# A second output bank, sums by slot, and seven block products for the values of an attention layer

## What is computed

```python
ada = jax.nn.silu(c) @ w_ada[i] + b_ada[i]
sh_m, sc_m, gt_m, sh_f, sc_f, gt_f = [a[:, None, :] for a in jnp.split(ada, 6, axis=-1)]
h = rms_norm(x, g_pre_mix[i]) * (1 + sc_m) + sh_m
y = token_mixer(h, ...)          # proj = h @ w_in; attention || gla; concatenated @ w_out
x = x + gt_m * rms_norm(y, g_post_mix[i])
h = rms_norm(x, g_pre_ffn[i]) * (1 + sc_f) + sh_f
y = hier_moe(h, ...)             # top-1 group, top-2 experts of 32
x = x + gt_f * rms_norm(y, g_post_ffn[i])
```

## Time and profile before

| | us |
|---|---|
| three runs | 1489.6, 1491.54, 1492.07; median 1491.54 |
| the profiled execution, time | 1491.1 |
| its span in the profile | 1489.3 |
| granted TensorE clock, mean | 0.932 |
| busy, of the span | PE 83%, DVE 50%, PEld 37%, ACT 14%, POOL 4% |
| chain that ended last | DMA 38%, PE 34%, SP's queue 17%, DVE 7%, ACT 2% |

### The profile page before, as it was taken

The page is one execution under the profiler, slowest core; times in us unless marked ns, Lnnn a source line. Parts: engine busy times, 40 slices in busy tenths (PEclk is TensorE's granted clock), DMA queues, the critical chain, the costliest instruction groups (busy, mean ns, idle before and its releaser), DMA issues.

```text
span 1489.3 us, 18989 instructions
## 1 busy us (share of the span) xinstructions
PE 1236.6 (83%) x7341; PEld 548.7 (37%) x7342; DVE 748.9 (50%) x1082; ACT 211.6 (14%) x491; POOL 52.5 (4%) x68
## 2 busy tenths in 40 slices
PE   4799999899999999876777677767767779999967
PEld 4687644654444453321222122222222223333322
DVE  5876257678674866443234223422432335555525
ACT  3011121222201041100000000000000001111103
POOL 0000300000110020000000000000000000000010
PEclk9899999999999999989899889988898899999989
DMA  9999979888899789999999999999999999999996
GB/s 354 392 383 385 353 296 379 312 334 302 322 408 386 275 329 392 426 424 428 425 425 427 427 428 424 426 427 427 423 428 426 427 423 428 427 425 426 428 427 269
DMA packets 102004, 583.51 MB, mean 392 GB/s; under 512 B 6656, under 2 KB 31536, under 8 KB 58192
## 3 DMA queue, kind: packets, MB, share of 16 engines
q1 hardware_dynamic: 98752, 572.81, 94.6%
q10 hardware_dynamic: 1664, 6.46, 1.1%
q0 software_dynamic: 1552, 3.75, 0.9%
HBM read 579.30 MB, written 3.69 MB: 391 GB/s over the span
## 4 chain that ended last, share of the span: by engine, by line
DMA 38%; PE 34%; SPq 17%; DVE 7%; ACT 2%; issue 1%; POOL 0%; ACTq 0%; DVEq 0%
DMA stream<-in_w 32%; PE ps L701 8%; SPq L544 6%; PE ps L913 5%; DMA stream<-in_w_ada 5%; SPq L563 4%; PE ps L786 4%; PE ps L967 4%; SPq L538 3%; PE ps L632 3%; SPq L479 2%; PE ps L698 1%; PE ps L874 1%; PE ps L819 1%; DVE wk L1053 1%
## 5 line engine op out<-in xcount | busy, mean ns | idle before, releaser
L913 PE MATMUL ps<-stream,wk 128*32 128x512 f32 x2304 | 323.5, 690 | 132.8 <-DMA stream<-in_w 131.9
L1365 DVE TENSOR_TENSOR acc<-ps,acc 128x2048 f32<-128x2048 f32 x37 | 84.8, 2292 | 430.7 <-PE ps L874 430.7
L913 PEld LDWEIGHTS ps<-stream,wk 128*32 128x32 f32 x2304 | 71.2, 118 | 372.3 <-issue 296.8
L967 PE MATMUL ps<-stream,cst 128*32 128x512 f32 x1152 | 152.1, 656 | 61.9 <-DMA stream<-in_w 61.8
L701 PE MATMUL ps<-stream 128*128 128x512 f32 x448 | 196.6, 594 | 0.3 <-PE ps L632 0.3
L632 PE MATMUL ps<-stream 128*128 128x256 f32 x512 | 120.7, 401 | 1.8 <-ACT stream L1510 1.8
L701 PEld LDWEIGHTS ps<-stream 128*128 128x128 f32 x448 | 83.6, 190 | 99.3 <-issue 99.2
L632 PEld LDWEIGHTS ps<-stream 128*128 128x128 f32 x512 | 102.9, 202 | 17.4 <-issue 1.9
L920 PEld LDWEIGHTS ps<-cst,wk 128*128 128x128 f32 x576 | 70.4, 193 | 62.8 <-issue 62.8
L1053 DVE SCALAR_TENSOR_TENSOR wk<-stream,cc,wk 128x768 f32<-128x768 f32 (+1 forms) x90 | 83.6, 929 | 11.4 <-DMA stream<-in_w_ada 8.8
L874 PE MATMUL ps<-wk,cst 32*128 32x512 f32 x592 | 87.9, 664 | 0.8 <-ACT wk L1681 0.8
(11 more groups left out here) (270 smaller groups left out, 986.5 us busy)
## 6 DMA issues: line engine op xcount, KB each, us to landing
stream<-in_w SPq DMA_DIRECT2D x190, 2048.0 KB, 40.9
stream<-in_w_ada SPq DMA_DIRECT2D x64, 1024.0 KB, 7.0
stream<-in_w_in SPq DMA_DIRECT2D x8, 4096.0 KB, 16.7
stream<-in_w_ada SPq DMA_DIRECT2D x64, 384.0 KB, 10.0
stream<-in_w_out SPq DMA_DIRECT2D x4, 4096.0 KB, 16.3
stream<-in_w_ada SPq DMA_DIRECT2D x16, 512.0 KB, 10.1
stream<-in_w_in SPq DMA_DIRECT2D x4, 2048.0 KB, 13.2
stream<-in_w_in SPq DMA_DIRECT2D x2, 3072.0 KB, 16.2
```

What stands on the lines that cost most here:

```text
L913: last = nc.tensor.matmul(bank(1 + m)[32 * g:32 * g + 32, :], xe[:, k + g, :], w13[m][:, k + g, :], start=(k == 0), stop=(k == KD - 4))
L967: last = nc.tensor.matmul(bank(2)[32 * g:32 * g + 32, :], hid[:, k, :], w2v[:, k, 512 * g:512 * g + 512], start=(k == 0), stop=(k == 3))
L1365: V.tensor_tensor(y4, ps[:, b0:b0 + 4, :], y4, ALU.add).then_inc(ysum_sb, 1)
```

## The change

- **Block products.** `BLOCK_UNITS = [4, 5]`: for each of the two value units the 256 by 2048 by 512 product is made of seven products of 128 by 1024 by 256 (8 matmuls of 256 columns each) in place of eight. TensorE makes two in three of the unit's slots and one in the fourth. VectorE forms four sums of h once (128 by 1024 each), and for each unit four sums of weight blocks (128 by 2048) in place, in the unit's slab, and eight sums of output blocks (128 by 256). ACT copies two of the products.
- **Second output bank.** `o_bank`: the outputs of `att` go to bank 4 and bank 6 in turn, four each, so the wait for `o_sb` before a new group is one group later. `mod_bank` is rearranged to make room.
- **Sums by slot.** `ADA_IN` gives for each of the 36 places how many `ada` items stand there. m = 2 ends in slot 13, m = 3 in slot 23, m = 4 in slot 32 (`wout` 0), and m = 5 has 5, 5 and 6 items at `wout` 1, 2 and 3. `partial` 4 and `mod` 4 stand behind the second `wout` item, `partial` 5 behind T2, `mod` 5 behind `prod` 4.
- **Later wait at the output unit.** The first `wout` item of each token block waits for the linear attention's transposed half at its ninth matmul and no longer at its first.

```diff
-ADA_AT = [0, 10, 20, 30, SLOTS + 3]
+ADA_IN = [0, 0, 1, 1, 1, 1, 1, 0, 2, 2, 1, 2, 2, 2, 0, 1, 1, 2, 2, 1, 2, 2, 2, 3, 0, 2, 2, 2, 2, 2, 2, 1, 3, 5, 5, 6]
+ADA_SLOT = [s for s, n in enumerate(ADA_IN) for _ in range(n)]
...
         if w == 0:
-            out += [("gmul", 1, 1), ("partial", 4), ("wout", 0, 0), ("glaT", 1), ("mod", 4)]
+            out += [("gmul", 1, 1), ("wout", 0, 0), ("glaT", 1)]
         else:
             out.append(("wout", w // 2, w % 2))
+            if w == 1:
+                out += [("partial", 4), ("mod", 4)]
         if w == 3:
             out.append(("mix", "S"))
-        out += [("ada", n) for n in range(48, 64) if ada_slot(n) == SLOTS + w]
...
+        out += [("ada", n) for n in range(32, 64) if ada_slot(n) == SLOTS + w]
+    out += [("prod", 0), ("mix", "T1"), ("prod", 1), ("mix", "C11"), ("mix", "T3"), ("prod", 2),
+            ("mix", "T2"), ("partial", 5), ("prod", 3), ("mix", "T4"), ("prod", 4), ("mod", 5), ("mix", "U2"), ("prod", 5), ("prod", 6)]
...
         def mod_bank(m):
-            return bank(3 if m == 4 else 6)
+            return bank({2: 5, 3: 3, 4: 3, 5: 6}[m])
+
+        def o_bank(j):
+
+            return bank(4 + 2 * (j // 4 % 2), 4, A_DV)[:, j % 4, :]
...
+                    def block_product(left, right, n):
+                        for k in range(8):
+                            last = nc.tensor.matmul(block_bank(b, n), left[:, k, :], right[:, k, :], start=(k == 0), stop=(k == 7))
+                        last.then_inc(blk_ps, 1)
...
-                        if j >= 4 and j % 4 == 0:
-                            pe.wait_ge(o_sb, j // 4)
+                        if j >= 8 and j % 4 == 0:
+                            pe.wait_ge(o_sb, j // 4 - 1)
...
-                    if u == 0:
-                        pe.wait_ge(glaT_sb, 2 * t + 2)
                     pe.wait_ge(proj_sb, fill - 1)
                     for k in range(KD):
+                        if u == 0 and k == 8:
+                            pe.wait_ge(glaT_sb, 2 * t + 2)
```

More of the change, by code:

```diff
@@ L153, in schedule @@
     beside[0] += [("alpha", 0), ("row",)]
-    beside[2] += [("alpha", 1), ("lam",)]
+    beside[1] += [("alpha", 1)]
+    beside[2] += [("decay",)]
+    beside[3] += [("lam",), ("tail", 0)]
+    beside[7] += [("tail", 1)]
     beside[4].append(("alpha", 2))
@@ L174, in schedule @@
     for s in range(SLOTS):
-        out.append(("proj",) + slot_unit(s))
+        i, half, part = slot_unit(s)
+        out.append(("block", i - 4, 2 * half + part) if i in BLOCK_UNITS else ("proj", i, half, part))
         out += beside[s]
@@ L358, in build, with quarter, h_block, out_block @@
         T1, T2, T3, T4 = B11, B22, B12, B21
+        def quarter(b, k, n):
+            return unit_w(b)[:, 8 * k:8 * k + 8, 256 * n:256 * n + 256]
+        def h_block(t, k):
+            return hT[:, 8 * k:8 * k + 8, P * t:P * t + P]
+        def out_block(b, t, n):
+            return va[:, t, 512 * b + 256 * n:512 * b + 256 * n + 256]
+        def block_bank(b, n):
+            return bank((0, 1, 6)[(7 * b + n) % 3])[:, 0:256]
+        hsum = [view(s3, 2048 + 1024 * i, 8, P) for i in range(4)]
         def ada_quarter(n):
@@ L693, in _ @@
                         pe.wait_ge(unit_in[i % 2], 16 * ((i - 4) // 2 + 1))
-                    if part == 0:
-                        pe.wait_ge(proj_sb, fill - 1 if fill > HELD + 1 else fill - HELD + 1)
+                    if part == 0 and fill > HELD + 1:
+                        pe.wait_ge(proj_sb, fill - 1)
+                    elif part == 0:
+                        pe.wait_ge(blk_out, 8 * len(BLOCK_UNITS) - 1 + fill - HELD)
                     if c in TRANSPOSED:
@@ L739, in _ @@
                         pe.wait_ge(o_sb, g + 1)
+                        if g == 1:
+                            pe.wait_ge(mod_sb, 1)
                         for j in range(4):
@@ new lines, in _, with w_sum, o_sum, block @@
+            h_sum(hsum[3], h_block(0, 0), h_block(1, 0), 4, ALU.subtract)
+            def w_sum(out_, in0, in1, n):
+                V.tensor_tensor(out_, in0, in1, ALU.subtract).then_inc(blk_t, 1)
+                dve.wait_ge(blk_t, n)
+            def o_sum(out_, in0, in1, n):
+                V.tensor_tensor(out_, in0, in1, ALU.add).then_inc(blk_out, 1)
+                dve.wait_ge(blk_out, n)
+            def block(b, part):
+                c11, c12, c21, c22 = [out_block(b, t, n) for t in range(TT) for n in range(2)]
+                if part == 0:
+                    dve.wait_ge(unit_in[b], 16)
+                    dve.wait_ge(blk_ps, 7 * b + 1)
+                    w_sum(quarter(b, 0, 0), quarter(b, 0, 1), quarter(b, 0, 0), 4 * b + 5)
+                    w_sum(quarter(b, 0, 1), quarter(b, 1, 1), quarter(b, 0, 1), 4 * b + 6)
+                elif part == 1:
+                    dve.wait_ge(blk_ps, 7 * b + 2)
+                    w_sum(quarter(b, 1, 1), quarter(b, 1, 1), quarter(b, 0, 0), 4 * b + 7)
+                    dve.wait_ge(blk_ps, 7 * b + 3)
+                    dve.wait_ge(blk_copy, 2 * b + 1)
+                    o_sum(c11, c12, block_bank(b, 2), 8 * b + 1)
+                    w_sum(quarter(b, 1, 0), quarter(b, 1, 0), quarter(b, 1, 1), 4 * b + 8)
+                elif part == 2:
+                    dve.wait_ge(blk_ps, 7 * b + 4)
+                    o_sum(c21, c12, block_bank(b, 3), 8 * b + 2)
+                    dve.wait_ge(blk_ps, 7 * b + 5)
+                    o_sum(c12, c12, block_bank(b, 4), 8 * b + 3)
+                    o_sum(c21, c21, block_bank(b, 4), 8 * b + 4)
+                else:
+                    dve.wait_ge(blk_ps, 7 * b + 6)
+                    dve.wait_ge(blk_copy, 2 * b + 2)
+                    o_sum(c12, c12, block_bank(b, 5), 8 * b + 5)
+                    o_sum(c12, c12, c22, 8 * b + 6)
+                    o_sum(c22, c21, block_bank(b, 5), 8 * b + 7)
@@ L1179, in _ @@
                     accumulate(item[1])
+                elif kind == "block":
+                    block(item[1], item[2])
+                elif kind == "tail":
+                    block_tail(item[1])
                 elif kind == "wout":
@@ L1552, in _ @@
                         A(st[:, 32:48], bank(7)[:, 0:16], ACT.Exp, scale=1.0 / GATE_TAU).then_inc(suf_exp, 1)
+                elif kind == "block":
+                    _, b, part = item
+                    if part == 0:
+                        if b == 0:
+                            act.wait_ge(stage_ps, len(STAGES))
+                        for n, out_ in ((0, out_block(b, 0, 1)), (1, out_block(b, 1, 1))):
+                            act.wait_ge(blk_ps, 7 * b + n + 1)
+                            A(out_, block_bank(b, n), ACT.Copy).then_inc(blk_copy, 1)
                 elif kind == "proj":
@@ L1590, in _ @@
                         for j in range(4):
-                            ins = A(tmp[:, 0:A_DV], bank(4, 4, A_DV)[:, j, :], ACT.Square, accum_out=st[:, 16 + j:17 + j])
+                            ins = A(tmp[:, 0:A_DV], o_bank(4 * g + j), ACT.Square, accum_out=st[:, 16 + j:17 + j])
                             if j < 3:
@@ L1599, in _ @@
                         for j in range(4):
-                            ins = A(on[:, j, :], bank(4, 4, A_DV)[:, j, :], ACT.Copy, scale=st[:, 20 + j:21 + j])
+                            ins = A(on[:, j, :], o_bank(4 * g + j), ACT.Copy, scale=st[:, 20 + j:21 + j])
                         ins.then_inc(o_sb, 1)
```

78 lines of the change are left out of this document (65 added, 13 removed).

## The result

The changed kernel takes **1498.32 us** (median of 7 runs, 1496.23 to 1500.18) against 1491.54 (7 runs, 1489.6 to 1492.07): ratio **1.0048**, 95% interval 1.0035 to 1.0061. It is slower, where 1486.5 us with a range of 1475 to 1493 had been forecast. The profiled execution took 1499.9 us, its span is 1498.1 and its mean granted clock 0.924 (0.932 before).

What follows compares the result with a forecast made beforehand. Bound by transfers in the experts' stretch and by TensorE before it. Products start 18.5 us earlier, 12.7 given back: 1491.1 - 5.8 + 0.8 = 1486.1, plus 0.4 for the runs' median: 1486.5 us, range 1475 to 1493.

Steps and rivals of the forecast that it cites:

- Block products: Two value units in the slots: seven products instead of eight, 24.2 us a unit in place of 27.6, -6.9 together.
- the rule that was weighed: Block products: if weight load and streaming added up, each pass would cost 0.19 more; rival at 1529, chance 0.01.
- Second bank and the 5.50 us: TensorE's idle at 278: bank alone wins nothing; VectorE's new order takes 5.0 off, and 2.1 of slower matmuls behind it.
- Later wait: First two `wout` items: the first eight matmuls cover the copies, removing idle times of 1.32 and 1.80 us, -3.1.
- E: The end of the attention slots on TensorE: 435.45 before, forecast at 420.0.
- Unit 11's load is held: SyncE's queue at the output products: issue waits until 487.7, landing at 502.4; TensorE idles 11.0 us before `prod` 2.
- the step from the fold to n = 59: VectorE after `mod` 4's fold, 449.9 to 487.7: work up to accumulation 59, after which load 63, then unit 11, may issue.
- serial: VectorE's work from 449.9 summed end to end, six `ada` at 2.44 each among it, reaching 487.7.
- the 0.8 allowed: Behind the products: first token block's norm follows on ACT ahead of the second's squares, about +0.8.
- The second rival: Held load binds harder: unit 11 takes 16.3 to 21.7, or VectorE waits for an `ada` behind unit 10; +2 to +7; 0.18.
- the 18.5 us: Gain up to the products' start, 477.6 against 496.09; the forecast gives back 12.7 of it by their end.

Runs made afterwards that it cites:

- no_blocks: The changed kernel with units 4 and 5 made as plain projections, without block products or VectorE's sums for them: 1504.71 us.
- light_rows: The changed kernel, order and operations untouched, loading only a quarter of each `ada` row of m = 5 (last gain not the reference's): 1485.72 us.
- light_paced: paced_reread with only a quarter of each `ada` row of m = 5 loaded, as in light_rows: 1482.98 us.
- paced_reread: paced with ScalarE's loads moved: x re-read behind its square sums (slot 28), the gain's broadcast behind the first output unit's eviction: 1486.16 us.
- paced: The changed kernel with `partial` 4 and `mod` 4 before the second `wout`, four `ada` rows back in the slots, unit 10 ahead of the last seven: 1486.45 us.

## Why the prediction was wrong

**Right, and now tested.** *Block products* -6.9: 32 passes of 256 columns take 7.14 and 80 take 17.43, 0.218 each, and no_blocks is 6.4 us slower. Those 17.43 us also bear on the rule that was weighed. The Trainium skill, TensorE: Matmul & The Clock Gate, section Back-to-back issue gap, has the spacing set by both operations of a pair. Read as a sum, that is not what this trace shows: the weight load of 0.19 us stays hidden behind 0.22. *Second bank and the 5.50 us*: "the bank alone wins nothing", the order of VectorE does (-5.0 - 2.1; measured 7.1). *Later wait* -3.1 (2.9). E was forecast at 420.0 and came at 419.2. The products were forecast to start at 477.6, and all that stands ahead of them on TensorE was done by 476.6.

**Right in kind.** Unit 11's load is held behind the sums of m = 5, and most of the gain is lost there. The fold, forecast to end at 449.9, was over at 448.8. That VectorE stands 14.8 us before it, and SyncE's queue and the transfers with it, follows from that time, but the prediction did not say so.

**Wrong: the step from the fold to n = 59.** The prediction summed VectorE's work from 449.9 to 487.7 "serial", with every row in its buffer when VectorE came to it. Measured, that work ended at 498.5: VectorE began 1.0 earlier, did 0.2 less of work, and stood twice for rows, 2.60 and 9.37. Unit 11 was issued 11.1 later than forecast and took 15.5 in place of 14.7, so product 2 began at 514.3 and not at 502.4. That is the whole miss at the products' end, 551.9 against 539.4, but for 0.6 us. Beside it stands an idle time that the forecast did not have, 7.24 before product 0, with the slower clock behind it (16.55 for 13.98); it is hidden by the wait for unit 11. The tail behind the products was 1.3 longer than the 0.8 allowed.

The chain that ended last, in order of time, shows the three loads that it passes through:

```profile
449.32 1.30 DVE wk L1239
450.63 9.91 DMA stream<-in_w_ada
460.57 2.35 DVE wk L1241
...
469.56 16.69 DMA stream<-in_w_ada
486.27 2.35 DVE wk L1241
...
498.78 15.44 DMA stream<-in_w_out
```

The first is row 52. With four buffers it can only be issued when VectorE is through with row 48, at 450.6, and it lands 9.9 us later beside ACT's 3 MB, while the three rows between them keep VectorE busy for 7.3: this wait, 2.60, has nothing to do with unit 10, which is issued at 463.3. The second is row 57, issued behind unit 10 and landing 16.7 us later. Unit 10's 4 MB, in a stretch that is full, cause this wait, 9.37, and the 7.24 before product 0 (light_rows, with unit 10 whole and the rows light, has 1.08 and none). The prediction has no term for them. It took unit 10 as there when it is needed. But its issue was held at the same place as everything else, and in the burst behind the dry stretch it took 20.4 us. The second rival named this very wait ("VectorE waits for an ada behind unit 10"), and gave it 2 to 7 us and 0.18. It measured 9.4, and it was the likelier course, as the bytes show that fall due from the fold on: ACT's 3 MB, five rows, unit 10 and row 57, 13 MB of 1.05 million bytes each, 34 us at the measured 402 GB/s, from 450 to 484 (row 57 was there at 486.3). That sum could have been made ahead of the result, with the rates of the earlier trace rows.

What is not settled is which plan would carry all of the 18.5 us. Mending the three causes one by one moved the wait about, to rows behind units 8 and 10 at last. Of what keeps light_paced at 1483, 6.5 us are the late fold of m = 4. ScalarE's loads, moved to 391 to 396 us in paced_reread and light_paced, are the larger part of that lateness (TensorE waits 5.37 for the sums in paced_reread, 1.69 in paced). No run has the paced order with these loads at a third place.

## What to carry to other kernels

When an edit makes one engine wait longer, follow what that wait stops on the in-order queues, and count the bytes that are then due at once: a transfer that was hidden is hidden only while the queue keeps running. Price a moved step by the whole stretch up to the next point where all engines meet, and not by the engine's busy time. A long stall before an engine can be the order of a few cheap instructions two engines away: two rows of 2.35 us, put behind a softmax instead of ahead of it, gave 7.1.
